# Position bias masks on one Trainium2 core: four masks ahead of the first slab splits, later splits earlier in the mask loop, latent norms moved up

## What is computed

```python
bias = rel_bias[_t5_bucket(dist)]                      # diff attention: dist = pos[q] - pos[k], 32 buckets, 4 heads
logits = einsum(q, k) * scale + bias
q  = _rmsnorm(c_q, q_norm) @ w_uq                      # MLA: c_q 256 wide, c_kv 128 wide
kv = _rmsnorm(c_kv, kv_norm) @ w_ukv
```

## Time and profile before

| | us |
|---|---|
| median of 3 runs | 3367.71 (3367.39 to 3368.2) |
| the profiled execution's own time | 3368.49 |
| span of its profile | 3366.6 |
| TensorE busy in it | 3304.8 (98%) |
| mean granted clock of TensorE | 0.996 of full speed |

### The profile page before, as it was taken

The page is one execution under the profiler, slowest core; times in us unless marked ns, Lnnn a source line. Parts: engine busy times, 40 slices in busy tenths (PEclk is TensorE's granted clock), DMA queues, the critical chain, the costliest instruction groups (busy, mean ns, idle before and its releaser), DMA issues.

```text
span 3366.6 us, 47171 instructions
## 1 busy us (share of the span) xinstructions
PE 3304.8 (98%) x20115; PEld 2685.1 (80%) x20115; DVE 1819.5 (54%) x3063; ACT 1290.9 (38%) x2160; POOL 118.6 (4%) x211
## 2 busy tenths in 40 slices
PE   8999998999999999999999999999999999999998
PEld 6878766888888888888668888888888877788887
DVE  6575764578766665665654533353333656453333
ACT  5233555435434422234553422242223455342222
POOL 1000000010000011100000000000000000000000
PEclk9999999999999999999999999999999999999999
DMA  4110112565544265643112222223232321222322
GB/s 149 38 47 25 38 48 69 172 206 181 188 150 150 102 236 194 236 165 111 51 45 88 94 99 95 94 94 100 94 99 95 114 79 45 82 94 94 100 94 69
DMA packets 101729, 364.09 MB, mean 108 GB/s; under 512 B 11776, under 2 KB 13888, under 8 KB 100880
## 3 DMA queue, kind: packets, MB, share of 16 engines
q1 hardware_dynamic: 77040, 272.14, 23.9%
q0 software_dynamic: 24480, 88.95, 8.0%
HBM read 358.94 MB, written 2.10 MB: 107 GB/s over the span
## 4 chain that ended last, share of the span: by engine, by line
PE 91%; DVE 5%; ACT 3%; issue 0%; DMA 0%; POOL 0%; DVEq 0%; ACTq 0%; POOLq 0%
PE ps_run L448 90%; PE ps_run L812 2%; DVE wl L2008 1%; ACT nrm L1230 1%; ACT wh L1230 1%; DVE nrm L2015 0%; DVE msk L2012 0%; PE ps_run L1081 0%; DVE HL L2015 0%; ACT HH L1230 0%; ACT bias L1230 0%; DVE X L2015 0%; DMA vec<-vec 0%; DVE At L2008 0%; DVE L L2223 0%
## 5 line engine op out<-in xcount | busy, mean ns | idle before, releaser
L448 PE MATMUL ps_run<-HH,wh 128*128 128x512 f32 (+1 forms) x2776 | 1067.7, 385 | 18.4 <-ACT nrm L1230 7.0
L448 PE MATMUL ps_run<-HH,wl 128*128 128x512 f32 (+1 forms) x2776 | 1047.9, 377 | 0.0
L448 PE MATMUL ps_run<-HL,wh 128*128 128x512 f32 (+1 forms) x2776 | 1047.6, 377 | 0.0
L2008 DVE TENSOR_TENSOR wl<-st,wh 128x1024 fp32r<-128x1024 f32 (+1 forms) x511 | 622.3, 1218 | 743.3 <-ACT wh L1230 743.2
L1230 ACT ACTIVATE wh<-st 128x1024 fp32r<-128x1024 f32 (+1 forms) x511 | 534.7, 1048 | 722.8 <-PE ps_run L448 721.0
L448 PEld LDWEIGHTS ps_run<-HH,wh 128*128 128x128 f32 x2776 | 524.1, 189 | 123.1 <-ACT nrm L1230 7.3
L448 PEld LDWEIGHTS ps_run<-HH,wl 128*128 128x128 f32 x2776 | 523.9, 189 | 96.9
L448 PEld LDWEIGHTS ps_run<-HL,wh 128*128 128x128 f32 x2776 | 524.5, 189 | 95.6 <-issue 3.8
L448 PE MATMUL ps_run<-AH,wh 128*128 128x512 f32 (+1 forms) x1167 | 445.8, 382 | 0.0
L448 PE MATMUL ps_run<-AL,wh 128*128 128x512 f32 (+1 forms) x1167 | 440.7, 378 | 0.0
L448 PE MATMUL ps_run<-AH,wl 128*128 128x512 f32 (+1 forms) x1167 | 440.6, 378 | 0.0
(11 more groups left out here) (422 smaller groups left out, 3325.4 us busy)
## 6 DMA issues: line engine op xcount, KB each, us to landing
st<-wst SPq DMA_DIRECT2D x511, 512.0 KB, 3.3
mb<-ada POOLq DMA_DIRECT2D x144, 512.0 KB, 4.7
cw<-cw POOLq DMA_DIRECT2D x4, 1024.0 KB, 6.2
X<-xT SPq DMA_DIRECT2D x8, 256.0 KB, 6.2
X<-xT POOLq DMA_DIRECT2D x8, 256.0 KB, 3.3
out<-X SPq DMA_DIRECT2D x16, 128.0 KB, 1.8
kc<-kc POOLq DMA_DIRECT2D x1, 1073.5 KB, 6.9
mb<-cond POOLq DMA_DIRECT2D x2, 512.0 KB, 6.5
```

What stands on the lines that cost most here:

```text
L448: i = self.e.matmul(out, lhsT, rhs, start=start, stop=stop, skip_group_check=True)
L2008: self.e.tensor_tensor(out, a, b, op).then_inc(*self.w.done(*points))
```

## The change

In `diff()`, VectorE writes four masks ahead of the two splits that stood behind mask 0. The other five splits of the stage, which stood behind masks 32, 64, 80, 96 and 112, now stand in `rel_bias` ahead of masks 28, 60, 76, 92 and 108. ScalarE's five copies stand in its own loop two steps earlier, at 26, 58, 74, 90 and 106. The latents' norms move from masks 60 to 82 up to masks 24 to 50. Nothing is added or removed; all instructions are the same.

```diff
@@ Pe.rel_bias
-            if g == 60:
+            if g == 24:
                 for i in range(2):
                     self.sums("q", i, 2, m.dPT, (4, 5))
@@ Act.rel_bias
-            if g == 64:
+            if g in (26, 58, 74, 90, 106):
+                finish(self.spend(8))
+            if g == 34:
                 self.root("q", m.dPT[3], 256)
                 self.root("kv", m.dPT[0], 128)
-            if g == 74:
+            if g == 44:
                 self.high("q", 2, m.prep, m.MH)
@@ Act.diff
         for i, dst in enumerate(m.dk):
-            finish(self.spend(8))
+            if i < 3:
+                finish(self.spend(8))
...
         for i in range(4):
-            finish(self.spend(8))
@@ Dve.rel_bias
-            if g == 72:
+            if g in (28, 60, 76, 92, 108):
+                finish(self.spend(8))
+            if g == 40:
                 self.latents_scaled()
-            if g == 82:
+            if g == 50:
                 self.latents_low()
@@ Dve.diff
         for i in range(4):
-            finish(self.spend(8))
-            for _ in range(32 if i >= 2 else 1 - i):
-                next(gb, None)
+            if i < 3:
+                finish(self.spend(8))
+            for _ in range((4, 0, 28, 32)[i]):
+                next(gb)
         for _ in range(4):
-            finish(self.spend(8))
             for k in range(16):
                 next(gb, None)
```

## The result

The changed kernel takes 3386.8 us (median of 4 runs, 3382.1 to 3388.1), the kernel before 3367.7 (median of 4). The profiled execution is the one of 3382.13 us, the fastest of the four, with a span of 3380.2.

A forecast was written before the change was run, and what follows sets the result against it. TensorE, busy for 98% of the span, was taken as the bound. New waits 14.6 + 2.1, less 4.6 removed, plus 3.4 of clock, gave 15.5 us on 3367.7: 3383.2, taken as 3383; range 3376.5 to 3389.

The forecast's parts named there:

- the forecast case: Bias stage: the new waits come, with one to three clock falls; 3380 to 3386 us, chance 62%.
- rival 2: Bias stage: all four long pauses bring a clock fall; 3386.6 us, to 3389 if one takes two; chance 13%.
- Part one: Four masks ahead of the first splits: mask 4 comes when it came, same 1.6 us idle; effect 0.
- Part two: Five later splits: VectorE waits for ScalarE's copy, so TensorE waits ahead of 28, 60, 76, 92, 108; 14.6 us lost.
- Part three: Latents' norms at their new place, and angles: new TensorE waits, 1.7 us at mask 40; sum 2.1 us.
- What is removed: Bias stage: all of TensorE's old mask waits but the first go, 3.6 us plus 1.0 of tails; 4.6 us gained.
- The clock: TensorE behind the four new long pauses: two clock falls of four, 3.4 us lost; bounds 0 and 6.8.

The follow-up runs named there:

- e4: The kernel before with only the four masks put ahead of the first two splits; 3368.0 us, ratio 1.0001.
- e1: The kernel before with only the five later splits moved, on VectorE and ScalarE; 3387.5 us, ratio 1.0060.
- e2: The changed kernel with only VectorE's five splits put back behind masks 32, 64, 80, 96 and 112; 3377.9 us, ratio 1.0021 to the kernel before.
- e3: The kernel before with only the latents' norms moved to masks 24 to 50; 3367.7 us, ratio 0.9999.
- e9: The changed kernel with 14 extra unused matmuls ahead of each of masks 60, 76, 92 and 108; 3379.2 us, ratio 1.0037 to the kernel before.
- e5: The changed kernel with VectorE's five splits two masks later, ScalarE's order unchanged; 3381.7 us, ratio 1.0051 to the kernel before.
- e7: The changed kernel run again unaltered, for a second profile; 3387.3 us, ratio 1.0058 to the kernel before.
- e10: e2 with 4 extra unused matmuls of 512 columns ahead of the latent attention's first scores; 3369.9 us, ratio 1.0006 to the kernel before.
- e11: e6 with 4 extra unused matmuls ahead of the latent attention's first scores; 3362.1 us, ratio 0.9985 to the kernel before.
- e8: e2 run again unaltered, for a second profile; 3369.5 us, ratio 1.0011 to the kernel before.
- e6: The changed kernel with VectorE's splits, scaled latents and angle steps placed where TensorE starts stretches without masks; 3362.7 us, ratio 0.9995 to the kernel before.

## Why the prediction was right, and where it was off

The forecast was 3383 us, slower by more than 0.2%; the median is 3386.8. That lies in the range, but above the 3380 to 3386 of the forecast case itself, and among the times of rival 2 (3386.6 to 3389).

**Part one** held: e4 is 1.0001 of the kernel before, and the pause of 1.50 us stands ahead of mask 4. VectorE works in order; what matters is the sum of the work ahead of the mask that TensorE lacks.

**Part two** held, the mechanism and the size. Waits of 0.5, 3.4, 3.55, 3.55 and 3.6 us were forecast; the profile has 0.30, 3.31, 3.21, 3.35 and 3.31, to which some 0.16 us of the previous matmul's tail must be added for each. e1 and e2 show that this part alone carries the loss, and that VectorE's places do; ScalarE's cost 1.1 us in one place where nothing hides it (e2), which the prediction did not have. VectorE's waits in front of the five splits were to be 2.5 to 3 us and are 1.4 to 2.3; at 76 the angle steps fill part of that time. TensorE's waits came out as forecast all the same.

**Part three** held: 1.70 us at mask 40 (forecast 1.7), 0.26 at 50 (0.2) and 0.15 at 84 for the angles (0.2). The forecast of 0.2 at 50 does not come out of the terms given for it: 1.8 us against 1.37 + 0.75 of cover leaves no wait; it takes the mask itself and a handover as well, which stand in the other sums. As a change of its own it was worth nothing that can be measured (e3).

**What is removed** held as a term: parts two and three less the old waits were to be 12.1 us, and e9, with the clock kept up, measures 12.1.

**The clock** was mis-sized. I took two falls of four, 3.4 us, by the two pauses of 2.24 and 2.71 us that had left it alone; e9 puts it at 7 to 8 us. Rival 2, a fall behind each of the four, came nearer with 3386.6 us. The Trainium skill (TensorE: Matmul & The Clock Gate, "HAM oscillation — how this bites in real kernels") says that each such pause is paid for. By that rule, the trace agrees in three pauses of four in the first profile and in all four in the second. The step that failed is the reading of two single pauses, in one execution, as a bound on pauses near them: e5 has a fall behind 2.03 us, and the pause of 2.24 us itself is followed by a fall in the profile of the changed kernel (0.76 from 219 to 226).

That the profiled run (3382.1 us) lies so near the forecast is in part luck. The prediction has two new falls and keeps the one behind the first pause, 3.4 us more than before. The profile has three new ones and has lost that one, which makes 3.4 us again. In the second profile (e7, 3387.6 us) the first fall is back and there are 8.5 us more than before.

Also not foreseen was that the clock's falls make the time scatter, as the two profiles of the changed kernel show. Its first four runs span 6 us and those of the kernel before 0.8, but in the 25 that ran later the kernel before spans 5.7 us too: that the change makes the scatter larger is not shown.

## What to carry to other kernels

When work is put into an in-order queue that feeds the bounding engine, ask not only how long it takes but what it waits for, and start it when the bounding engine begins a stretch that does not need this queue. Here the split had to wait for ScalarE, which the same event had just given 1.2 to 2.4 us of other work; five masks earlier in the list meant 3.3 us later on TensorE. And count a pause of TensorE twice, once for its length and once for the clock that may fall behind it, 1.7 us for most falls here and twice that for some. Whether it falls differs from one execution to the next, so look at more than one profile before a pause is called harmless. Where a pause can't be avoided, matmuls whose results nobody uses keep the clock up; fitted to the pause, they cost nothing in e9 and 0.16 us in e10.

## What the runs showed of the hardware that was not expected

- The same kernel with the same waits (17.1 us in two profiles) lost 5.1 us of clock in its stage in one execution and 10.2 in the other.
- A pause of 2.03 us can bring the clock down (e5), and one of 2.71 us can pass (kernel before, 564 to 572 us). The same pause in unchanged work does either: that of 2.2 us near 222 brought a fall in four of 13 profiles, that of 2.7 us near 568 in four.
- Once down at the start of the latent attention, the clock stayed at 0.51 for 21 us while TensorE was busy throughout, 8.1 us lost. The matmuls of its scores have 64 or 32 rows where the slabs' have 128; whether that keeps the clock low was not tested. With four matmuls of 512 columns in the pause ahead of it, 0.9 us, it stayed up in both profiles and none of 22 runs lay in the upper group (e10, e11); without them it was down in both profiles of e2 and e8, and 12 of the 25 runs of e2, e8 and e6 lay in an upper group 8 to 10 us above the others.
